# Holding splits back behind evictions in an expert layer, with down weights loaded as row pairs

## The chip, the cores and the metric

The kernel runs on one core of a Trainium2 chip. A core has five engines with queues of their own, which meet through semaphores: TensorE (PE, matrix products and transposes into PSUM), VectorE (DVE), ScalarE (ACT), GpSimd (POOL) and SyncE (SP, which here issues loads). Sixteen DMA engines move data between HBM and SBUF. The metric is the device time of one execution in microseconds, lower is better.

## What is computed

A trunk of two layers over 256 tokens of width 1024, all in float32. Each layer has a mixer (three attention-like branches); layer 0 then has a dense feed-forward block and layer 1 a mixture of 8 experts. The change touches the experts alone:

```python
def swiglu(h, w_gate_up, w_down):
    gt, up = jnp.split(h @ w_gate_up, 2, axis=-1)
    return (jax.nn.silu(gt) * up) @ w_down

def moe_swiglu(h, w_router, w_gate_up, w_down):   # D_FF_EXPERT = 3584, N_EXPERTS = 8, TOP_K = 2
    ...
    for e in range(N_EXPERTS):
        y = y + combine[:, e:e + 1] * swiglu(t, w_gate_up[e], w_down[e])
```

## The kernel before

**Two parts for each weight.** To keep float32 precision a weight slab is split: ACT copies it to a rounded high part (`exp_hi`, L1104), DVE subtracts that from the raw slab to get the low part (`exp_lo`, L1618), and PE multiplies with both.

**Slots.** The experts run in slots, one expert each. A slot gathers the tokens of its expert, multiplies, and scatters the result. Slots 0, 1, 3, 5, 7 are big (up to 128 tokens; three products per weight tile: hi x hi, hi x lo, lo x hi, `passes`, L1895 to L1897). Slots 2, 4, 6 are small (`few`, up to 64 tokens): there the tokens' high and low parts lie side by side in one operand, so PE needs two products per tile (L2231, L2232), and the half that holds the low part is folded in by `low` on ACT and `fold_low` on PE. In this data there are 8 slots; the last one is a turn of a loop that is written for up to 11.

**Slabs.** The weights of an expert come as 42 slabs of 128 x 2048 float32, 1 MiB each. An expert's hidden width is cut in four steps, three of 1024 columns and one (step 3) of 512. The order of the slabs, from 0, is: step 0 gate (0 to 3) and up (4 to 7); step 1 gate (8 to 11) and up (12 to 15), down of step 0 (16 to 19); step 2 gate and up (20 to 27), down of step 1 (28 to 31); step 3 gate (32, 33) and up (34, 35), down of step 2 (36 to 39), down of step 3 (40, 41). SP loads them into 14 raw places in turn (L555); a load waits until PE has used the slab 14 before. The high parts have a ring of 6 places (`EXP_RING`): ACT may split slab j once PE has used slab j - 6, its "holder". The numbering runs on over slots: slab 0 of a slot follows slab 41 of the one before.

**Evictions.** Beside splits, ACT and DVE carry the results on: `silu` (ACT, L1147) and the product with the up half, `hidden` (DVE, `hs`, L1744); `hidden_hi` and `hidden_lo` (`hts`, L1154 and L1753), which take the transposed hidden values out of PSUM, and `hts_end` for step 3; `y_hi` (L1165) and `output_lo` (L1711) for the result of the slot before; `add_slot` (`xs`, L1719) after the scatter; `tokens_hi` and `tokens_lo` (`xg`, L1116 and L1640) for the tokens of the next slot. PE transposes `hs` in `turn_hidden` (L2260) once DVE has made it (`e_h`), and in a small slot `block(1, 1, ...)`, the up product of step 1, waits for the `hs` of step 0 too, because it writes where DVE reads.

**What sets the order.** ACT and DVE run the same hand-written program: `uses(n)` counts slabs that PE will have used (`used`), and at each count `expert_split` puts in all splits that are allowed by then: those whose holder is below `used - LATE`. An eviction stands where the count reaches the slabs it needs, and waits for PE there. With `LATE` = 1 the splits up to slab `used` + 4 stand ahead of it in the queue. An instruction that waits holds up all that is queued behind it on its engine.

**Loads of the down weights.** Slab q of the down matrix takes 256 rows of 1024 columns. Partition p gets the rows p and 128 + p of them, each 4 KB, as two k-tiles. PE transposes `hs[:, a*P:(a+1)*P]` to make the matching hidden columns a k-tile.

Of the kernel before, what the change touches and what calls it, by code (L numbers as in the profile page):

```python
# [30 lines left out]
P = 128  # L31
# [25 lines left out]
EXP_SLAB = 2048  # L57
EXP_RAW, EXP_RING, LATE = 14, 6, 1

# [39 lines left out]
def is_first(i):  # L99
    return type(i) is int and i == 0  # L100


# [93 lines left out]
def trunk(nc, x_in, mem_in, mix_norm_g, w_in, sb_q_g, sb_k_g, gla_a_up, gla_a_b, gla_o_g, ca_q_g,  # L196
# [10 lines left out]
    with ExitStack() as ctx:  # L207
# [315 lines left out]
        def _(sp):  # L523
# [12 lines left out]
            def expert_slabs(e, i):  # L536
                gate_up = moe_gate_up[0].rearrange("e (k p) n -> e p k n", p=P)
                down = moe_down[0].rearrange("e (k p) n -> e p k n", p=P)
                j = 0

                def load(src, n):
                    nonlocal j
                    if not is_first(i) or j >= EXP_RAW:
                        sp.wait_ge(slab_used, i * EXP_SLABS + (PRE + j - EXP_RAW + 1))
                    if j == W_RAW_SLOT:
                        sp.wait_ge(lo_ready, PRE)
                    if j == GATES_SLOT:
                        sp.wait_ge(norm_done, NT * (3 * LAYERS))
                    if j == XT_SLOT:
                        sp.wait_ge(slab_used, PRE)  # L550
                    if j == HN_SLOT:
                        sp.wait_ge(gathered, 1)
                        sp.wait_ge(h_stored, 16)
                    dst = exp_slots[j % EXP_RAW].rearrange("p (k n) -> p k n", k=n)
                    sp.dma_start(dst, src).then_inc(more_ready[j % EXP_RAW], 16)  # L555
                    j += 1

                def cols(c, w):
                    n = EXP_SLAB // w
                    for k in range(0, KT, n):  # L560
                        load(gate_up[bass.ds(e, 1), :, k:k + n, c:c + w]
                             .rearrange("e p k n -> p (e k) n"), n)

                def rows(s):
                    c, w = STEP[s]
                    n = EXP_SLAB // DM
                    for k in range(c // P, (c + w) // P, n):
                        load(down[bass.ds(e, 1), :, k:k + n, :].rearrange("e p k n -> p (e k) n"),
                             n)

                for s, (c, w) in enumerate(STEP):
                    cols(c, w)
                    cols(D_EXP + c, w)
                    if s > 0:
                        rows(s - 1)
                rows(STEPS - 1)
# [239 lines left out]
        def _(act):  # L816
# [275 lines left out]

            def expert_split(i, few, used):

                nonlocal j
                while j < EXP_SLABS:
                    if RINGS[few][j] is not None:
                        place, holder = RINGS[few][j]
                        if holder >= used - LATE:
                            return  # L1100
# [20 lines left out]

            def expert(i, few, next_few, folds=0):
                nonlocal j
# [3 lines left out]
                def uses(n):  # L1127
                    nonlocal used
                    for _ in range(n):
                        used += 1  # L1130
                        expert_split(i, few, used)

# [29 lines left out]
                if not is_first(i):  # L1162
                    expert_split(i, few, 0)
                    act.wait_ge(slab_used, at + PRE)
# [40 lines left out]
            for i in range(1, 7, 2):  # L1205
                expert(i, False, True)
                expert(i + 1, True, False, i * STEPS)
            with act.Fori(7, slots) as i:
                expert(i, False, False)
            act.wait_ge(slab_used, slots * EXP_SLABS + PRE)  # L1210
# [5 lines left out]
        def _(dve):  # L1216
# [392 lines left out]

            def expert_split(i, few, used, at_most=EXP_SLABS):  # L1610
                nonlocal j
                while j < at_most:
                    if RINGS[few][j] is not None:
                        place, holder = RINGS[few][j]
                        if holder >= used - LATE:
                            return
# [5 lines left out]

            expert_split(0, False, 0, 1)
            link(dve.memset(slot_pos, 0.0))
# [98 lines left out]

            def expert(i, few, next_few, folds=0):
                nonlocal j
# [3 lines left out]
                def uses(n):  # L1729
                    nonlocal used  # L1730
                    for _ in range(n):
                        used += 1
                        expert_split(i, few, used)
                        if is_first(i):
# [33 lines left out]
                if not is_first(i):  # L1768
                    expert_split(i, few, 0)
                    output_lo(i)  # L1770
# [51 lines left out]
            for i in range(1, 7, 2):  # L1822
                expert(i, False, True)
                expert(i + 1, True, False, i * STEPS)
            with dve.Fori(7, slots) as i:
                expert(i, False, False)
            for c in range(2):
# [8 lines left out]
        def _(pe):  # L1836
# [385 lines left out]
            def expert(i, few, folds=0):  # L2222
# [25 lines left out]
                def fold_low(s, up):  # L2248
# [5 lines left out]
                    ins.then_inc(low_folded, 1)  # L2254

                def turn_hidden(s):
                    pe.wait_ge(e_h, i * STEPS + (s + 1))
                    dst = ps[:, DM:2 * DM] if s < STEPS - 1 else pa[:, BW:2 * BW]
                    for a in range(STEP[s][1] // P):
                        ins = pe.transpose(dst[:, a * P:(a + 1) * P], hs[:, a * P:(a + 1) * P],  # L2260
                                           ident[:, :])
# [117 lines left out]
```

## Time and profile before

| | us |
|---|---|
| median of 3 runs | 1708.3 (1707.7 to 1708.5) |
| profiled execution | 1706.9 |
| its span | 1705.0 |
| experts (from the first `exp_hi` to the end) | about 766 to 1705 |
| slot 4, small | about 1248 to 1351 |
| slot 5, big | about 1351 to 1473 |

The span is what the trace covers, from its first instruction to its last; a few microseconds lie around it. In the rows further down, a timeline row has its start, its duration, the engine, the line and what it writes and reads, and in brackets how long the engine had been idle before and who released it. Instructions overlap a little in an engine: the next one starts about 0.1 us before the last one's end, so work is counted from start to start.

### The profile page before, as it was taken

The page shows a single profiled execution, that of the slowest core. Times are in us where ns is not written, and L with a number is a line of the kernel's source. Part 1 is how long each engine was busy: PE and PEld are TensorE (multiplying, and loading weights), DVE is VectorE, ACT ScalarE, POOL GpSimd, SP SyncE. Part 2 cuts the span into 40 slices and gives each one's busy share as a digit, 9 for nine tenths or more (in the row PEclk, how much of TensorE's full clock was granted, in tenths as well). Part 3 has the DMA queues.
Part 4 walks back from the last instruction along what each step waited for, and adds up shares of the span by engine and source line. Part 5 has one row for each costly group of instructions (what it writes and reads, how often), then busy time and mean ns, then how long its engine had stood idle before and what let it go on. Part 6 is the DMA issues. An engine that isn't in the chain of part 4 may idle for free.

```text
span 1705.0 us, 20144 instructions
## 1 busy us (share of the span) xinstructions
PE 1627.2 (95%) x7594; PEld 1332.1 (78%) x7594; DVE 1305.4 (77%) x965; ACT 1108.9 (65%) x950; POOL 104.5 (6%) x123
## 2 busy tenths in 40 slices
PE   7999998999999999978999998899989899988998
PEld 5777886888887778867888887688877788876886
DVE  6654666555666546658989889999899998999985
ACT  5547554444555565536777778887698877887773
POOL 4111000000012110000200000000000000000000
PEclk9999999999999999998999999999999999999999
DMA  8544444656565544487999999999999999999990
GB/s 275 179 142 147 149 148 154 216 184 187 175 209 162 148 149 148 148 322 265 370 384 354 377 367 401 400 409 405 386 381 396 409 409 403 384 403 409 409 385 26
DMA packets 161335, 484.84 MB, mean 284 GB/s; under 512 B 12992, under 2 KB 15072, under 8 KB 161248
## 3 DMA queue, kind: packets, MB, share of 16 engines
q1 hardware_dynamic: 158112, 474.16, 76.2%
q0 software_dynamic: 3136, 9.48, 1.6%
q8 instruction: 60, 0.98, 0.2%
q14 instruction: 27, 0.22, 0.0%
HBM read 481.50 MB, written 2.10 MB: 284 GB/s over the span
## 4 chain that ended last, share of the span: by engine, by line
PE 83%; DVE 11%; issue 2%; ACT 2%; POOL 1%; DMA 0%; DVEq 0%; POOLq 0%; ACTq 0%
PE pa L1895 18%; PE pa L1897 18%; PE pa L1896 18%; PE ps L1997 5%; DVE exp_lo_a L1618 5%; PE ps L1895 4%; PE ps L1897 4%; PE ps L1896 4%; PE pa L2231 3%; PE pa L2232 3%; DVE exp_lo_b L1618 2%; PE ps L2260 1%; PE ps L2231 1%; PE ps L2232 1%; POOL hrs L697 1%
## 5 line engine op out<-in xcount | busy, mean ns | idle before, releaser
L1618 DVE TENSOR_TENSOR exp_lo_a<-exp_raw_a,exp_hi 128x2048 fp32r<-128x2048 f32 x240 | 538.3, 2287 | 35.2 <-ACT exp_hi L1104 34.9
L1104 ACT ACTIVATE exp_hi<-exp_raw_a 128x2048 fp32r<-128x2048 f32 x240 | 451.4, 1918 | 90.9 <-PE pa L1897 50.0
L1232 DVE TENSOR_TENSOR w_lo<-w_raw,w_hi 128x1024 fp32r<-128x1024 f32 (+2 forms) x229 | 277.4, 1226 | 135.8 <-ACT w_hi L830 126.9
L830 ACT ACTIVATE w_hi<-w_raw 128x1024 fp32r<-128x1024 f32 (+2 forms) x229 | 237.3, 1050 | 171.7 <-PE pa L1897 147.6
L1895 PE MATMUL pa<-w_hi,r 128*128 128x512 f32 x600 | 240.0, 400 | 0.0
L1897 PE MATMUL pa<-w_hi,r 128*128 128x512 f32 x600 | 234.0, 390 | 0.0
L1896 PE MATMUL pa<-w_lo,r 128*128 128x512 f32 x600 | 233.8, 390 | 0.0
L1618 DVE TENSOR_TENSOR exp_lo_b<-exp_raw_b,exp_hi 128x2048 fp32r<-128x2048 f32 x96 | 217.9, 2288 | 15.4 <-ACT exp_hi L1104 14.5
L1895 PE MATMUL pa<-exp_hi,xg 128*128 128x512 f32 x560 | 220.4, 394 | 3.4 <-issue 3.4
L1897 PE MATMUL pa<-exp_hi,xg 128*128 128x512 f32 x560 | 218.7, 391 | 0.0
L1104 ACT ACTIVATE exp_hi<-exp_raw_b 128x2048 fp32r<-128x2048 f32 x96 | 182.6, 1918 | 31.6 <-PE pa L1897 23.6
L2231 PE MATMUL pa<-exp_hi,xg 128*128 128x512 f32 x336 | 139.6, 415 | 14.2 <-issue 14.2
L1896 PE MATMUL pa<-exp_lo_a,xg 128*128 128x512 f32 x380 | 148.4, 390 | 0.0
L1895 PE MATMUL pa<-w_hi,xt 128*128 128x512 f32 (+1 forms) x320 | 124.2, 388 | 9.5 <-DVE xt L1268 9.5
L1895 PEld LDWEIGHTS pa<-w_hi,r 128*128 128x128 f32 x600 | 112.7, 188 | 25.6 <-issue 2.0
L1897 PEld LDWEIGHTS pa<-w_hi,r 128*128 128x128 f32 x600 | 112.6, 188 | 24.3
L1896 PEld LDWEIGHTS pa<-w_lo,r 128*128 128x128 f32 x600 | 112.8, 188 | 21.9
L1895 PEld LDWEIGHTS pa<-exp_hi,xg 128*128 128x128 f32 x560 | 105.5, 188 | 24.8 <-issue 3.6
L1897 PE MATMUL pa<-w_hi,xt 128*128 128x512 f32 (+1 forms) x320 | 122.8, 384 | 0.0
L1897 PEld LDWEIGHTS pa<-exp_hi,xg 128*128 128x128 f32 x560 | 105.4, 188 | 22.1
L1896 PE MATMUL pa<-w_lo,xt 128*128 128x512 f32 (+1 forms) x320 | 122.6, 383 | 0.0
L1895 PE MATMUL ps<-exp_hi,hts 128*128 128x512 f32 x240 | 94.5, 394 | 0.0
(299 smaller groups left out, 2269.4 us busy)
## 6 DMA issues: line engine op xcount, KB each, us to landing
exp_raw_a<-in_moe_w_gate_up SPq DMA_DIRECT2D x152, 1024.0 KB, 9.6
exp_raw_a<-in_moe_w_down SPq DMA_DIRECT2D x88, 1024.0 KB, 8.9
exp_raw_b<-in_moe_w_gate_up SPq DMA_DIRECT2D x72, 1024.0 KB, 8.4
w_raw<-in_w_in SPq DMA_DIRECT2D x104, 512.0 KB, 4.3
exp_raw_b<-in_moe_w_down SPq DMA_DIRECT2D x24, 1024.0 KB, 8.7
w_raw<-in_ff_w_gate_up SPq DMA_DIRECT2D x44, 512.0 KB, 4.5
w_raw<-in_ff_w_down SPq DMA_DIRECT2D x22, 512.0 KB, 3.5
w_raw<-in_w_mem_kv SPq DMA_DIRECT2D x16, 512.0 KB, 5.8
```

What stands on the lines that cost most here:

```text
L697: pool.tensor_tensor(dst[:, 0:n], src[:, 0:n], half[:, 0:n], ALU.pow)\
L830: act.activation(w_hi[:, s % SPLIT, 0:n], raw_slot(s)[:, 0:n], ACT.Copy)\
L1104: act.activation(exp_hi[:, place, :], exp_slots[j % EXP_RAW], ACT.Copy)\
L1232: dve.tensor_tensor(w_lo[:, s % SPLIT, 0:w], raw_slot(s)[:, 0:w], w_hi[:, s % SPLIT, 0:w].bitcast(F32), ALU.subtract)\
L1618: dve.tensor_tensor(exp_lo[j % EXP_RAW], exp_slots[j % EXP_RAW], exp_hi[:, place, :].bitcast(F32), ALU.subtract)\
L1895: pe.matmul(dst, hi, m_hi, start=first, stop=False)
L1896: pe.matmul(dst, hi, m_lo, start=False, stop=False)
L1897: return pe.matmul(dst, lo, m_hi, start=False, stop=last)
L1997: return pe.matmul(dst, a, b, start=start, stop=stop, skip_group_check=True)
L2231: pe.matmul(dst, src[:, 0, k, :], m_hi, start=first, stop=False)
L2232: return pe.matmul(dst, src[:, 0, k, :], m_lo, start=False, stop=last)
L2260: ins = pe.transpose(dst[:, a * P:(a + 1) * P], hs[:, a * P:(a + 1) * P], ident[:, :])
```

## The change

Three edits, all in the experts.

1. `LATE` is replaced by a number that depends on the slot and on `used`. A split is put in while its holder is below `used - late`, so with `late` = L the splits up to slab `used` + 5 - L are ahead of an eviction. In a small slot L is 1 up to `used` = 9, 2 to 19, 3 to 29, 4 to 39 and 5 at the end. In a big slot behind a small one it is 5 up to `used` = 7, 4 to 15, 3 to 23, 2 to 31 and then 1. Slots 0 and 1 keep 1.
2. A down slab gives partition p the neighbouring rows 2p and 2p + 1 of its 256, one run of 8 KB.
3. To match, `turn_hidden` transposes columns with a step of two: for an even a the even columns of a block of 256, for an odd a the odd ones.

```diff
+def holds_back(few, after_few, used):
+
+    if few:
+        return 1 + used // 10
+    return max(1, 5 - used // 8) if after_few else 1
...
-                down = moe_down[0].rearrange("e (k p) n -> e p k n", p=P)
+                down = moe_down[0].rearrange("e (q p k) n -> e p q (k n)", p=P, k=EXP_SLAB // DM)
...
-                    n = EXP_SLAB // DM
-                    for k in range(c // P, (c + w) // P, n):
-                        load(down[bass.ds(e, 1), :, k:k + n, :].rearrange("e p k n -> p (e k) n"),
-                             n)
+                    n = EXP_SLAB // DM * P
+                    for q in range(c // n, (c + w) // n):
+                        load(down[bass.ds(e, 1), :, q:q + 1, :].rearrange("e p q n -> p (e q) n"),
+                             1)
...
-            def expert_split(i, few, used):
+            def expert_split(i, few, used, late=1):
...
-                        if holder >= used - LATE:
+                        if holder >= used - late:
...
-                        expert_split(i, few, used)
+                        expert_split(i, few, used, holds_back(few, after_few, used))
...
-                    expert_split(i, few, 0)
+                    expert_split(i, few, 0, holds_back(few, after_few, 0))
...
-                expert(i, False, True)
+                expert(i, False, True, after_few=i > 1)
...
-                expert(i, False, False)
+                expert(i, False, False, after_few=True)
...
+                row_pairs = hs[:, :].rearrange("p (q c k) -> p q k c", c=P, k=EXP_SLAB // DM)
...
-                        ins = pe.transpose(dst[:, a * P:(a + 1) * P], hs[:, a * P:(a + 1) * P],
+                        ins = pe.transpose(dst[:, a * P:(a + 1) * P], row_pairs[:, a // 2, a % 2, :],
```

The edits of `expert_split` and of `uses` are made alike in ACT's and in DVE's program. Instructions are neither added nor taken away.

DVE, the end of small slot 4 and the start of big slot 5. `exp_lo` rows are splits, L1744 is `hs` (1024 wide for step 2, 512 for step 3), L1711 is `output_lo`, L1719 is `add_slot`. Before:

```order
L1618 TENSOR_TENSOR exp_lo_a<-exp_raw_a,exp_hi 128x2048 x6
L1618 TENSOR_TENSOR exp_lo_b<-exp_raw_b,exp_hi 128x2048
L1618 TENSOR_TENSOR exp_lo_a<-exp_raw_a,exp_hi 128x2048
L1744 TENSOR_TENSOR hs<-pa,hs 128x1024
L1618 TENSOR_TENSOR exp_lo_a<-exp_raw_a,exp_hi 128x2048 x2
L1753 TENSOR_TENSOR hts<-ps,hts 128x8x64
L1618 TENSOR_TENSOR exp_lo_b<-exp_raw_b,exp_hi 128x2048 x2
L1744 TENSOR_TENSOR hs<-pa,hs 128x512
L1618 TENSOR_TENSOR exp_lo_b<-exp_raw_b,exp_hi 128x2048
L1753 TENSOR_TENSOR hts_end<-pa,hts_end 128x4x64
L1640 TENSOR_TENSOR xg<-ps,xg 128x1024
L1618 TENSOR_TENSOR exp_lo_a<-exp_raw_a,exp_hi 128x2048 x5
```

And now (the lines of the file are 7 further down):

```order
L1625 TENSOR_TENSOR exp_lo_a<-exp_raw_a,exp_hi 128x2048 x6
L1751 TENSOR_TENSOR hs<-pa,hs 128x1024
L1625 TENSOR_TENSOR exp_lo_a<-exp_raw_a,exp_hi 128x2048
L1625 TENSOR_TENSOR exp_lo_b<-exp_raw_b,exp_hi 128x2048
L1760 TENSOR_TENSOR hts<-ps,hts 128x8x64
L1625 TENSOR_TENSOR exp_lo_a<-exp_raw_a,exp_hi 128x2048 x2
L1751 TENSOR_TENSOR hs<-pa,hs 128x512
L1625 TENSOR_TENSOR exp_lo_a<-exp_raw_a,exp_hi 128x2048
L1760 TENSOR_TENSOR hts_end<-pa,hts_end 128x4x64
L1647 TENSOR_TENSOR xg<-ps,xg 128x1024
L1625 TENSOR_TENSOR exp_lo_b<-exp_raw_b,exp_hi 128x2048 x3
```

Ahead of the `hs` of step 2 stood splits up to slab 36, now up to 33; ahead of `hts_end` up to 41, now up to 38.

ACT at the same seam: `exp_hi` rows are splits, L1165 is `y_hi`, which waits for slab 41 of the small slot, and the L1147 behind it is `silu` of step 0 of the big slot, which waits for slab 3. Before:

```order
L1154 ACTIVATE hts_end<-pa 128x4x64
L1104 ACTIVATE exp_hi<-exp_raw_a 128x2048 x5
L1165 ACTIVATE hts<-ps 128x1024
L1104 ACTIVATE exp_hi<-exp_raw_a 128x2048 x2
L1104 ACTIVATE exp_hi<-exp_raw_b 128x2048
L1104 ACTIVATE exp_hi<-exp_raw_a 128x2048
L1147 ACTIVATE hs<-pa 128x1024
```

And now:

```order
L1161 ACTIVATE hts_end<-pa 128x4x64
L1111 ACTIVATE exp_hi<-exp_raw_b 128x2048 x3
L1111 ACTIVATE exp_hi<-exp_raw_a 128x2048
L1172 ACTIVATE hts<-ps 128x1024
L1111 ACTIVATE exp_hi<-exp_raw_a 128x2048 x4
L1154 ACTIVATE hs<-pa 128x1024
```

Ahead of `y_hi` stood the splits of slabs 0 to 4 of the big slot, now that of slab 0 alone (the three ahead of it are 39 to 41 of the small slot); ahead of `silu` slabs up to 8, now up to 4.

## Rows read from the trace of the kernel before

**Rows 1.** The page, section 1: busy us, share of the span, instructions.
```profile
PE 1627.2 (95%) x7594; PEld 1332.1 (78%) x7594; DVE 1305.4 (77%) x965; ACT 1108.9 (65%) x950; POOL 104.5 (6%) x123
```

**Rows 2.** PE's waits, 780 to 1705 us: total us, times, longest us.
```profile
PE ps L2260 <- DVE hs L1744: 16.9, 3, 5.6
PE pa L2231 <- issue: 14.2, 3, 4.8
PE pa L1895 <- issue: 3.4, 1, 3.4
```

**Rows 3.** DVE's timeline, slot 4: start, us, instruction, [idle before].
```profile
1240.14 11.10 DVE L1618 TENSOR_TENSOR exp_lo_a<-exp_raw_a,exp_hi 128x2048 fp32r<-128x2048 f32 x5 [1.00 <-ACT exp_hi L1104]
...
1276.69 1.22 DVE L1744 TENSOR_TENSOR hs<-pa,hs 128x1024 f32<-128x1024 f32 x1
...
1289.37 4.49 DVE L1618 TENSOR_TENSOR exp_lo_a<-exp_raw_a,exp_hi 128x2048 fp32r<-128x2048 f32 x2 [1.66 <-ACT exp_hi L1104]
...
1313.30 13.29 DVE L1618 TENSOR_TENSOR exp_lo_a<-exp_raw_a,exp_hi 128x2048 fp32r<-128x2048 f32 x6
...
1342.40 2.29 DVE L1618 TENSOR_TENSOR exp_lo_b<-exp_raw_b,exp_hi 128x2048 fp32r<-128x2048 f32 x1 [0.18 <-ACT exp_hi L1104]
1344.61 0.42 DVE L1753 TENSOR_TENSOR hts_end<-pa,hts_end 128x256 fp32r<-128x256 f32 x1
...
1346.07 11.09 DVE L1618 TENSOR_TENSOR exp_lo_a<-exp_raw_a,exp_hi 128x2048 fp32r<-128x2048 f32 x5
```

**Rows 4.** PE's timeline, slots 4 and 5.
```profile
1278.01 0.76 PE L2231 MATMUL pa<-exp_hi,xg 128*128 128x512 f32 x1 [4.74 <-issue]
...
1304.93 1.04 PE L2260 MATMUL ps<-ident,hs 128*128 128x128 f32 x8
1305.73 0.48 PE L2231 MATMUL pa<-exp_hi,xg 128*128 128x512 f32 x1
...
1309.90 0.39 PE L2231 MATMUL pa<-exp_hi,xg 128*128 128x512 f32 x1
...
1313.30 0.39 PE L2232 MATMUL pa<-exp_lo_b,xg 128*128 128x512 f32 x1
...
1361.77 1.98 PE L1997 MATMUL ps<-hts,selT 128*128 128x512 f32 x8
1363.58 0.39 PE L1895 MATMUL pa<-exp_hi,xg 128*128 128x512 f32 x1
```

**Rows 5.** ACT's waits, 800 to 1700 us, the longest of eleven.
```profile
ACT exp_hi L1104 <- PE pa L1897: 62.2, 76, 1.8
```

**Rows 6.** Line 1711, `output_lo`, once a slot: ns min/median/max, first and last start.
```profile
L1711 DVE TENSOR_TENSOR hts<-ps,hts x7: 1216/1219/1220, 906.4 to 1581.0; 128x1024 fp32r<-128x1024 f32 x7
```

**Rows 7.** ACT's timeline, slot 4 and the start of slot 5.
```profile
1281.86 1.91 ACT L1104 ACTIVATE exp_hi<-exp_raw_a 128x2048 fp32r<-128x2048 f32 x1 [4.39 <-PE pa L2232]
...
1344.07 9.12 ACT L1104 ACTIVATE exp_hi<-exp_raw_a 128x2048 fp32r<-128x2048 f32 x5
1353.08 1.02 ACT L1165 ACTIVATE hts<-ps 128x1024 fp32r<-128x1024 f32 x1
1353.98 3.72 ACT L1104 ACTIVATE exp_hi<-exp_raw_a 128x2048 fp32r<-128x2048 f32 x2
...
1361.97 1.03 ACT L1147 ACTIVATE hs<-pa 128x1024 f32<-128x1024 f32 x1 [0.66 <-PE pa L1897]
```

**Rows 8.** By stretch: us, PE, PEld, DVE, ACT, POOL busy, PEclk, DMA share, GB/s.
```profile
782.70:786.00 3.30, 3.29 (x9) 2.64 (x10) 2.56 (x5) 0.00 (x0) 0.00 (x0) 0.57 0.28 113
1278.00:1285.00 7.00, 6.99 (x19) 5.48 (x20) 7.00 (x6) 1.91 (x1) 0.00 (x0) 0.58 1.03 410
1300.00:1308.00 8.00, 8.00 (x41) 6.72 (x40) 8.00 (x6) 8.00 (x7) 0.99 (x1) 1.00 1.05 393
1316.00:1340.00 24.00, 18.18 (x79) 14.05 (x78) 24.00 (x13) 17.83 (x14) 0.00 (x0) 0.93 1.03 410
```

**Rows 9.** Line 555, the loads issued from 1325 to 1330 us.
```profile
L555 SPq DMA_DIRECT2D exp_raw_a<-in_moe_w_gate_up x2: 2154/2154/2154, 1325.2 to 1327.6; - x2
...
DMA to landing us min/median/max: 18.5/18.5/18.6
```

More of the change, by code:

```diff
@@ L57 @@
 EXP_SLAB = 2048
-EXP_RAW, EXP_RING, LATE = 14, 6, 1
+EXP_RAW, EXP_RING = 14, 6
 FF_BLOCKS = [(c, min(BW, D_FF - c)) for c in range(0, D_FF, BW)]
@@ L1120, in _, with expert @@
             tokens_hi(1, False)
-            def expert(i, few, next_few, folds=0):
+            def expert(i, few, next_few, folds=0, after_few=False):
                 nonlocal j
@@ L1608, in _, with expert_split @@
             j = 0
-            def expert_split(i, few, used, at_most=EXP_SLABS):
+            def expert_split(i, few, used, late=1, at_most=EXP_SLABS):
                 nonlocal j
@@ L1614, in expert_split @@
                         place, holder = RINGS[few][j]
-                        if holder >= used - LATE:
+                        if holder >= used - late:
                             return
@@ L1621, in expert_split @@
                     j += 1
-            expert_split(0, False, 0, 1)
+            expert_split(0, False, 0, at_most=1)
             link(dve.memset(slot_pos, 0.0))
@@ L1722, in add_slot, with expert @@
                         .then_inc(added, 1)
-            def expert(i, few, next_few, folds=0):
+            def expert(i, few, next_few, folds=0, after_few=False):
                 nonlocal j
@@ L1732, in uses @@
                         used += 1
-                        expert_split(i, few, used)
+                        expert_split(i, few, used, holds_back(few, after_few, used))
                         if is_first(i):
@@ L1768, in expert @@
                 if not is_first(i):
-                    expert_split(i, few, 0)
+                    expert_split(i, few, 0, holds_back(few, after_few, 0))
                     output_lo(i)
@@ L1822, in _ @@
             for i in range(1, 7, 2):
-                expert(i, False, True)
+                expert(i, False, True, after_few=i > 1)
                 expert(i + 1, True, False, i * STEPS)
             with dve.Fori(7, slots) as i:
-                expert(i, False, False)
+                expert(i, False, False, after_few=True)
             for c in range(2):
```

## The prediction

> **What bounds the kernel now.** The profiled execution took 1706.9 us for a span of 1705.0, beside a median of 1708.3 in the runs, so I work out a difference in the span and put it on 1708.3. The page's first section [rows 1] shows a busy TensorE (PE) for the whole span; a busy PE is not yet a bound, so the waits come next. In the experts PE waits in few places [rows 2]: once for 3.4 us at their start, and in each of the three small slots twice: 4.7 us (14.2 in all) at `block(1, 1, ...)` and 5.6 us (16.9) at `turn_hidden(2)`. The first is called "issue", but PE stands there before `e_h`, and it resumes at 1278.01 [rows 4], 0.1 us after DVE's `hidden(0)` ends (1276.69, 1.22 us) [rows 3]. So both stalls have one form: DVE's product `hs` stands in its queue behind splits of slabs that PE does not need yet. No wait of ACT in the experts names a DMA [rows 5]: no weight load is late.
>
> The second thing to read is DVE in the same slot [rows 3]. From 1240.14 (slab 0) to 1346.07 it is idle for 1.66 and 0.18 us alone. Six splits take 13.29 us, 2.20 apart. PE needs 0.227 us a matmul (1309.90 to 1313.30 for 15 steps) [rows 4], so 8 of them, 1.81 us, for a slab in a small slot, and 12, 2.72 us, in a big one. **A small slot is DVE's, a big one is PE's.** A stall of PE in a small slot is therefore mostly slack which it would have to spend elsewhere waiting for splits, and its length is not what removing it is worth. A pair of slots lasts (1581.0 - 906.4) / 3 = 224.9 us [rows 6].
>
> **The small slot after the change.** I follow slot 4; all three small slots show the same two stalls. With `late` = 1, DVE has split up to slab used + 4 when it comes to an eviction; with `late` = L up to used + 5 - L. That moves one split (2.2 us) behind `hidden(0)` and three (6.6 us) behind `hidden(2)`. No split is added or taken away.
> - Stall 1: `hs` starts at 1276.69 - 2.20 = 1274.5, PE resumes at 1275.8 and not at 1278.0. At full clock it does 2 slabs, one fold (0.45) and 8 transposes (0.9) by 1280.9, where it was 1286.0 before. ACT's wait of 4.39 us for PE ahead of slab 18 [rows 7] shrinks, and DVE's 1.66 us before slab 18 is gone: gain 1.7 us on DVE.
> - Stall 2: the six splits from 1313.30 are slabs 29 to 34, so slab 33 was split at 1324.3; now at 1324.3 - 1.7 = 1322.6, `hs` follows at once, PE ends slab 33 at 1324.6 and turns with no stall. What is late next is each split: 34 at 1325.9, 35 at 1328.1, after `hts` (half a `xg`, 0.6) 36 and 37 at 1330.9 and 1333.1. PE, which took 34 to 36 from stock before, now follows DVE at 2.2 us a slab.
> - End: `hs` of step 3 (0.6), 38, then `hts_end` and `xg`, 39, 40, 41. In the trace split 41 ends at 1344.6 [rows 3]. To this add those two evictions, which are now ahead of it (1346.07 - 1344.61 = 1.46), subtract the two idle times (1.84): 1344.2, and with 0.1 us of hand-over PE ends slab 41 at 1346.2.
> - Before: `hs` at 1361.97 waited for slab 3 of the next slot [rows 7], so PE ended it at 1361.8, and slab 41 four slabs earlier, at 1350.9. **Lead at the seam: 4.7 us.** It can't be the 10.4 us of both stalls, since DVE's sum ends there.
>
> **The big slot after it.** `late` starts at 5 here, and each eviction that must wait for PE now has little behind it in stock. The trace of before has no such wait, so I price it by the durations of its steps.
> - used = 0: only slab 0 is split (1346.5; PE starts it 0.3 late). ACT's `y_hi` (0.92 to its next instruction [rows 7]) waits for slab 41 and slab 1's high part stands behind it: 1346.2 + 0.1 + 0.9 + 1.9 + 0.1 = 1349.2, low part 2.2: 1351.4. PE has been done with slab 0 since 1349.3: **a new stall of 2.1 us**. Before, five slabs lay ready ahead of `y_hi` (1346.07, x5).
> - used = 4: ACT's `silu(0)` waits for slab 3, DVE's `add_slot` for the scatter (8 matmuls, 1.81 us [rows 4]) with only slab 4 split. Behind the second half's scatter come 0.1 + 1.25 + 2.2 = 3.6 us, PE has slab 4 for 2.7: stall 0.9, with the start of DVE's first addition counted 1.2.
> - used = 12: slabs 12 and 13 are ready, `hts` hi, `silu`, hi 14 and lo 14 follow the transposes by 1.0 + 0.9 + 1.9 + 2.3 + 0.1 = 6.2 us against 5.4 of PE: stall 0.7.
> - used = 16 on: at least 2 slabs ahead and cheaper waits, DVE gains 0.5 us a slab: nothing.
>
> Of 4.7 us, 0.3 + 2.1 + 1.2 + 0.7 = 4.3 are given back: **0.4 us a pair, 1.3 us in all.** The big slot is PE's, so what is left of the lead goes through to the end.
>
> **Clock.** Behind the 3.4 us stall PE was granted 0.57 of its clock (near 1.2 GHz) for some 3 us, behind stall 1 0.58 [rows 8]; seven matmuls at 0.43 and not 0.227 cost 1.4 us. Stall 1 is now 2.5 us, the new one 2.1. For these I take nothing as the centre and 1.4 us each as the end of the range; in the small slot such a dip also restores up to 1.7 us of DVE's idle time.
>
> **Loads.** 14 of 42 loads of a slot read 8 KB rows in place of two 4 KB rows; their number, order and semaphores stay. Streaming 4 KB rows the engines moved 410 GB/s at share 1.03; where 2 KB rows (step 3) were among them 393 at 1.05 [rows 8]. If doubling once more gave as much again, a load of 2.56 us would fall by 0.11, 112 loads by 12 us of DMA time. None of it is on the path: the loads issued from 1325.2 to 1327.6 landed 18.6 us later at the latest [rows 9], by 1346.2, and are slabs 4 and 5 of the next slot, which ACT reached at 1351.3 and 1354.0 [rows 7]. The change reaches slab 4 near 1352.7. A pair moves 84 slabs of 1 MiB (128 x 2048 fp32), 215 us at 410 GB/s, under 224.9. So 0. What the trace can't exclude is that the row pairs are slower; they may be so by some 7 us of lag before ACT sees it. The Trainium skill (Perfetto Trace Analysis, DMA Optimizations) says that batching from 2 to 4 or 8 KB can dramatically improve throughput, when DMA-bound. By that rule up to the 12 us above would be gained; ACT's waits say that its condition isn't met, and it is a rival below.
>
> **Transposes.** 28 a slot read every second column of `hs`. Eight contiguous ones take 0.80 us to the next matmul (1304.93 to 1305.73) [rows 4]. No row of the kernel has a strided operand on PE. Ends: 0, and double, 0.1 us each, 28 x 5 big slots = 14 us (in small ones DVE hides it). I take 0, as only the weight load's read changes, and it overlaps matmuls. The Trainium skill (SBUF — State Buffer, Door 1: The DMA port swizzle) states 16-byte lines with at least two hits each for full rate: a step of two fp32 has exactly two, so by the page it costs nothing; no run here shows it yet.
>
> **Rivals.**
> - *Lead kept.* If the hold-back in big slots hardly bites (ACT or DVE further ahead than my walk has them, other hand-overs), 4.4 us a pair stay: -13 us, 1695. Half of it: 1702. For: before, not one stall of PE in a big slot after the first. Against: the order puts `y_hi` behind one split. Chance 0.25.
> - *Loads bind* in a way that no row names: all 12 us of DMA time come off, 1696. For: the engines are at share 1.03 for most of a small slot. Against: the releasers. Chance 0.02.
> - *Slower: stalls at the seam.* The stalls of 2.1 and 1.2 us cut PE's clock in the PE-bound slot, and the dip at stall 1 gives DVE its 1.7 us of idle back: 0.4 - 1.4 - 0.5 - 1.7 = -3.2 a pair, +10 us: 1718; with one of these, 1712. It decides once the dips cost over 0.4 us a pair. For: rows 8 after 3.4 us. Against: nothing shows a dip after 2 us. Chance 0.20.
> - *Strided transposes at half rate:* +14: 1721. Chance 0.06.
> - *The change doesn't do what it says* (the splits are held back, but some other wait is behind the stalls): 1708.3, inside the forecast's own range and chance.
>
> **How the numbers follow.** Forecast 0.47: 1708.3 - 1.3 = 1707. Its own range is 1702 to 1711 (0.5 us either way on each of three stalls a pair). 0.2%, 3.4 us, is about what a measurement can tell. Faster: lead kept 0.25, loads 0.02, plus 0.07 of the forecast: 0.34. Slower: 0.20 + 0.06 less 0.02: 0.24. Within: 0.42. For 8 in 10 the range goes from 1697 (most of the kept lead) to 1715 (most of the seam's price).
>
> **What would show it.** PE's waits for `hs`: 5.6 us x3 gone, the unnamed one 4.7 to 2.5. Small slots with PE at 2.2 us a slab to the end. Slab 41 of slot 4 ended 4.7 us earlier relative to its start. Then new PE waits in slots 3, 5 and 7: about 2 us before the second slab and 1 us at the sixth. A pair of 224.5 us. ACT's waits with no DMA, down loads landing no later. `hs` transposes at 0.8 us for eight. I am wrong if big slots show no new wait (then near 1695), if PE's clock falls at the seams, or if a DMA is named as releaser.

## The result

The changed kernel takes 1717.2 us (median of 5 runs, 1716.19 to 1717.58); the kernel before took 1708.27 beside it (1707.38 to 1708.51). The ratio is 1.0054, interval 1.0042 to 1.0066: slower by 9 us, where I had forecast 1 us faster and a range up to 1715. The profiled execution has a span of 1715.4 us against 1705.0. What stands ahead of the first transposes of `hs` in slot 0 varies by up to 4.5 us from one traced execution to another, whatever the kernel (they start between 816.5 and 821.0 us); so where I compare traces below, a "lag" is a start time less that in the kernel before, both counted from those transposes.

In the new file all names of the text keep their names, and their lines move by 7 or 9: splits L1104 and L1618 are L1111 and L1625, `y_hi` L1165 is L1172, `output_lo` L1711 is L1718, `hidden` L1744 is L1751, transposes L2260 are L2269.

The page of the changed kernel, section 1, answers to [rows 1]: the same instructions, and PE busy for 7 us more with no matmul added.
```profile
PE 1634.5 (95%) x7594; PEld 1328.8 (77%) x7594; DVE 1303.7 (76%) x965; ACT 1105.3 (64%) x950; POOL 104.4 (6%) x123
```
PE's waits in the experts, which answer to [rows 2] (us in total, times, longest):
```profile
PE pa L1902 <- DVE exp_lo_a L1625: 12.5, 10, 2.5
PE pa L2238 <- issue: 7.5, 3, 2.5
PE ps L2238 <- DVE exp_lo_b L1625: 5.9, 5, 1.9
PE pa L1902 <- issue: 4.9, 1, 4.9
```
The waits for `hs` (16.9 us) are gone and the unnamed ones fell from 4.7 to 2.5, both as forecast. In their place stands PE's wait for low parts in the big slots (12.5), and a second kind (5.9) that I had not priced, at the last slabs of the small slots. PE's timeline at the seam from slot 4 to slot 5 has all of them:
```profile
1345.28 0.50 PE L2238 MATMUL ps<-exp_hi,hts 128*128 128x512 f32 x1 [1.83 <-DVE exp_lo_b L1625]
1345.61 0.40 PE L2239 MATMUL ps<-exp_lo_b,hts 128*128 128x512 f32 x1
...
1346.48 0.63 PE L2238 MATMUL ps<-exp_hi,hts 128*128 128x512 f32 x1
1346.91 0.63 PE L2239 MATMUL ps<-exp_lo_b,hts 128*128 128x512 f32 x1
1347.34 0.63 PE L2238 MATMUL ps<-exp_hi,hts 128*128 128x512 f32 x1
...
1357.88 0.50 PE L1902 MATMUL pa<-exp_hi,xg 128*128 128x512 f32 x1 [2.53 <-DVE exp_lo_a L1625]
...
1366.17 1.98 PE L2004 MATMUL ps<-hts,selT 128*128 128x512 f32 x8
...
1372.01 0.50 PE L1902 MATMUL pa<-exp_hi,xg 128*128 128x512 f32 x1 [1.14 <-DVE exp_lo_a L1625]
```
The reader is to see three things: slab 39 waits 1.83 us; from 1346.48 the matmuls start 0.43 us apart and not 0.23; then slab 1 of the big slot waits 2.53 us and slab 5 waits 1.14. Slab 14 waits 0.67 (not shown). The other two seams have 2.10 and 2.14, 1.14 and 1.27, 0.67 and 0.67.

ACT's timeline at the same seam, answering to [rows 7]:
```profile
1346.40 1.89 ACT L1111 ACTIVATE exp_hi<-exp_raw_a 128x2048 fp32r<-128x2048 f32 x1
1352.67 1.03 ACT L1172 ACTIVATE hts<-ps 128x1024 fp32r<-128x1024 f32 x1 [4.38 <-PE ps L2239]
1353.60 7.31 ACT L1111 ACTIVATE exp_hi<-exp_raw_a 128x2048 fp32r<-128x2048 f32 x4
1366.37 1.03 ACT L1154 ACTIVATE hs<-pa 128x1024 f32<-128x1024 f32 x1 [5.47 <-PE pa L1904]
```
and DVE's, answering to [rows 3]:
```profile
1349.55 2.28 DVE L1625 TENSOR_TENSOR exp_lo_a<-exp_raw_a,exp_hi 128x2048 fp32r<-128x2048 f32 x1
1353.73 1.23 DVE L1718 TENSOR_TENSOR hts<-ps,hts 128x1024 fp32r<-128x1024 f32 x1 [1.90 <-ACT hts L1172]
1355.53 8.90 DVE L1625 TENSOR_TENSOR exp_lo_a<-exp_raw_a,exp_hi 128x2048 fp32r<-128x2048 f32 x4 [0.57 <-ACT exp_hi L1111]
1367.28 2.48 DVE L1726 SCALAR_TENSOR_TENSOR xs<-ps,small,xs 128x1024 f32<-128x1024 f32 x2 [2.85 <-PE ps L2004]
```
Before, five slabs were split ahead of `y_hi`, and ACT came to it with PE done. Now ACT stands 4.38 us before it with one slab behind it in stock, DVE stands 1.90 us, and both then split slab 1 while PE waits: the walk of the prediction for `used` = 0, step by step. DVE stands idle for 5.3 us at this seam in all (1.90, 0.57 and 2.85).

By stretch, answering to [rows 8] (us, busy times, PEclk, DMA share, GB/s):
```profile
1346.00:1350.00 4.00, 4.00 (x13) 3.10 (x12) 4.00 (x3) 2.30 (x2) 0.00 (x0) 0.57 1.02 409
1130.00:1134.00 4.00, 4.00 (x12) 3.14 (x13) 4.00 (x2) 2.89 (x2) 0.00 (x0) 0.63 1.02 409
1585.00:1588.00 3.00, 3.00 (x9) 2.33 (x8) 3.00 (x3) 1.51 (x1) 0.00 (x0) 0.51 1.03 410
1372.00:1376.00 4.00, 3.99 (x17) 3.30 (x18) 4.00 (x2) 4.00 (x3) 0.00 (x0) 1.00 1.02 423
```
The first three are one stretch from each seam: PE was granted 0.51 to 0.63 of its full clock there, so for most of each stretch it was at the lower of its two levels, 1.2 and not 2.4 GHz. I counted the 512-column matmuls that start about 0.43 us apart, from slot 2 on, and what they take over 0.227 us. **Before there were five such dips, 9.0 us in sum, every one inside a small slot, where PE has slack. In the changed kernel there are six, 8.7 us, but three of them, 4.5 us, lie at the seams** (1131 to 1134: 1.40; 1346 to 1349: 1.57; 1585 to 1588: 1.55). Two of these stand in the PE-bound big slot, behind the wait for slab 1. The one at 1346 stands in the last slabs of the small slot, behind the wait for slab 39, and is hidden in part: it cost about 0.9 us (see the lead at slab 41 below). The time at the low clock did not grow; it moved to where it is paid for.

### The profile page after: what moved, and what is told of

Read it like the earlier page. It is cut to its first block, busy times and chain, and to the rows that moved or that the text cites. A ratio compares the mean times of both kernels' runs of the same rounds, so it can differ in the third digit from the quotient of the medians.

```text
span 1715.4 us, 20144 instructions
## 1 busy us (share of the span) xinstructions
PE 1634.5 (95%) x7594; PEld 1328.8 (77%) x7594; DVE 1303.7 (76%) x965; ACT 1105.3 (64%) x950; POOL 104.4 (6%) x123
## 4 chain that ended last, share of the span: by engine, by line
PE 80%; DVE 12%; ACT 3%; issue 3%; POOL 1%; DMA 0%; DVEq 0%; ACTq 0%; POOLq 0%
PE pa L1902 18%; PE pa L1904 17%; PE pa L1903 17%; DVE exp_lo_a L1625 6%; PE ps L2004 5%; PE ps L1902 4%; PE ps L1904 4%; PE ps L1903 4%; PE pa L2238 3%; PE pa L2239 3%; DVE exp_lo_b L1625 2%; ACT exp_hi L1111 1%; PE ps L2269 1%; POOL hrs L704 1%; PE ps L2238 1%
## 5 line engine op out<-in xcount | busy, mean ns | idle before, releaser
L1625 DVE TENSOR_TENSOR exp_lo_a<-exp_raw_a,exp_hi 128x2048 fp32r<-128x2048 f32 x240 | 537.4, 2285 | 31.5 <-ACT exp_hi L1111 31.3
L1111 ACT ACTIVATE exp_hi<-exp_raw_a 128x2048 fp32r<-128x2048 f32 x240 | 448.4, 1913 | 51.2 <-PE pa L1904 30.1
L1902 PE MATMUL pa<-exp_hi,xg 128*128 128x512 f32 x560 | 223.2, 399 | 17.5 <-DVE exp_lo_a L1625 12.5
L1625 DVE TENSOR_TENSOR exp_lo_b<-exp_raw_b,exp_hi 128x2048 fp32r<-128x2048 f32 x96 | 216.8, 2286 | 9.5 <-ACT exp_hi L1111 9.2
L1111 ACT ACTIVATE exp_hi<-exp_raw_b 128x2048 fp32r<-128x2048 f32 x96 | 181.3, 1914 | 24.5 <-PE pa L1904 16.5
```

What stands on the lines that cost most here:

```text
L1111: act.activation(exp_hi[:, place, :], exp_slots[j % EXP_RAW], ACT.Copy)\
L1625: dve.tensor_tensor(exp_lo[j % EXP_RAW], exp_slots[j % EXP_RAW], exp_hi[:, place, :].bitcast(F32), ALU.subtract)\
L1902: pe.matmul(dst, hi, m_hi, start=first, stop=False)
```

## The experiments

**Which part does it.** Four kernels from the changed one: the row pairs alone (no hold-back), the hold-back alone, and the hold-back in one kind of slot alone. The runs below were timed in three sets, each beside the kernel before, which took 1707.57, 1707.58 and 1708.17 us in them; so medians of different sets compare to about 0.6 us.

*Row pairs and strided transposes alone (rows_only).* Edit, against the changed kernel:
```
-    if few:
-        return 1 + used // 10
-    return max(1, 5 - used // 8) if after_few else 1
+    return 1
```


> Edits 2 and 3 alone (8 KB row pairs and transposes with a step of two; every eviction has the splits of before ahead of it). Theory: the rise to 1717.2 is the hold-back's; the strided transposes cost 0.08 us for eight, as the changed kernel's slots 0 and 1 show (a lag of 1.33 us at the end of two slots, 0.66 of it at the start), so 8 slots give about +2 us over before: 1710 to 1711. Rival A (the row pairs speed up the loads, and loads matter): below 1708. Rival B (the row pairs or the stride carry most of the rise): 1714 or more.

Measured: 1711.06 (1709.53 to 1712.02; before 1707.57), ratio 1.0017 (1.0009 to 1.0026). Lag at the last scatter 3.0 us. They cost something.

*Hold-back alone (hold_only).* Edit, with the load's lines of the kernel before likewise:
```
-    ins = pe.transpose(dst[:, a * P:(a + 1) * P], row_pairs[:, a // 2, a % 2, :],
+    ins = pe.transpose(dst[:, a * P:(a + 1) * P], hs[:, a * P:(a + 1) * P],
```


> Edit 1 alone, with the 4 KB rows and contiguous transposes of before. Theory (edits add): 1717.2 less the 2 us of edits 2 and 3: about 1715. Rival A (8 KB rows help where the engines are saturated): 1717 or more. Rival B (the stride hurts in the PE-bound seams): 1710.

Measured: 1716.0 (1710.24 to 1716.94), ratio 1.0037 (1.0024 to 1.0051), final lag 5.9. Most of the loss is the hold-back's. The two edits do not simply add: alone they cost 8.4 and 3.5 us, together 8.9. The six runs also lie apart: two took 1710.2 and 1711.5 us at a mean granted clock of 0.989 and 0.990, four took 1715.8 to 1716.9 at 0.986 to 0.988. This fits dips at the seams that come in some executions and not in others, but only one of the six has a trace (1716.2; dips at 1132 and 1347, none at the third seam), so it is not shown.

*Small slots alone (small_only).* Edit:
```
-    return max(1, 5 - used // 8) if after_few else 1
+    return 1
```


> The changed kernel with the hold-back in small slots alone; big slots have the splits of before. Theory (the stalls at slab 1, 5 and 14 of the big slots come from holding back there): PE's lead of 2.4 us at slab 41 is kept in each of three pairs, less 0.3 for transposes, and the 1.3 us of slots 0 and 1 stay: about 1703, no new wait of PE in slots 3, 5, 7. Rival (DVE has no stock at the end of a small slot, and the stalls come from that whatever the big slot does): 1708 to 1714 with waits at slab 1 still there.

Measured: 1698.21 (1697.98 to 1699.35), ratio 0.9945 (0.9932 to 0.9958). Against rows_only this is 12.9 us less, 4.3 a pair, close to the forecast's lead of 4.7 and more than I expected here. PE's waits have the small slots' two kinds, and of the big slots' only one of 0.2 us:
```profile
PE pa L2238 <- issue: 7.5, 3, 2.5
PE ps L2238 <- DVE exp_lo_b L1625: 6.0, 5, 1.9
PE pa L1902 <- issue: 4.2, 1, 4.2
```
The lead does go through to the end when nothing takes it. This is what the rival "lead kept" said, with the hold-back in big slots removed rather than harmless.

*Big slots alone (big_only).* Edit:
```
     if few:
-        return 1 + used // 10
+        return 1
```


> The changed kernel with the hold-back in big slots alone. Theory: each of three seams costs a stall of about 2.5 us at slab 1, 1.3 at slab 5 and 1.0 at slab 14 with the restart, nothing is gained in small slots, 1.5 to 2 us for the transposes: 1708.3 + 14.4 + 2 = about 1725. Rival (the seams stall only because small slots end without stock): about 1710.

Measured: 1731.05 (1730.17 to 1731.3), ratio 1.0136 (1.0121 to 1.015): 20.0 us over rows_only, 6.7 a seam, as the changed kernel is 19.0 over small_only, 6.3 a seam. The three parts nearly add up: +3.5 for the rows, -12.9 small, +20.0 big make +10.6; measured 9. Its trace has the low clock at 1366 and 1598, in slots 5 and 7, behind waits of 2.53 us for slab 1, beside that of its small slots; behind the same wait of 2.53 us in slot 3 it has none.

**Which part of the big slots' schedule.** The prediction priced 2.1 + 0.3 at slab 1 and 1.2 + 0.7 later. Two kernels add one or the other to small_only:
```
-    return 1
+    return 5 if after_few and used == 0 else 1                     # seam_first
+    return max(1, 5 - used // 8) if after_few and used > 0 else 1  # seam_rest
```
*Only at used = 0 (seam_first).* 

> small_only, and in the big slots behind small ones a hold-back at their very start alone (late = 5 at used = 0, then 1). Theory: the wait of PE ahead of slab 1 (2.1 us), its restart and the clock dip behind it in the PE-bound slot cost 3.5 us a seam where the lead was kept: 1698.2 + 3 x 3.5 = 1708.7, and PE has no wait at slabs 5 and 14. Rival: only the named wait is lost, without the clock: 1698.2 + 3 x 2.1 = 1704.5. Other rival: what is not split ahead of slab 1 is missing later as well, and slab 5 stalls even at late = 1: up to 1712.

Measured: 1708.62 (1707.48 to 1710.46), 10.4 over small_only, 3.5 a seam. PE's timeline has the wait ahead of slab 1 at each seam (2.06, 2.09, 2.11) and none at slabs 5 and 14. The first two:
```profile
1130.13 0.50 PE L1902 MATMUL pa<-exp_hi,xg 128*128 128x512 f32 x1 [2.06 <-DVE exp_lo_a L1625]
...
1352.47 0.50 PE L1902 MATMUL pa<-exp_hi,xg 128*128 128x512 f32 x1 [2.09 <-DVE exp_lo_a L1625]
```
Behind the second the clock fell, behind the first it didn't, as the stretches show (PEclk is the third number from the end):
```profile
1130.00:1134.00 4.00, 3.87 (x17) 3.23 (x18) 4.00 (x3) 4.00 (x3) 0.00 (x0) 1.00 1.03 410
1354.00:1358.00 4.00, 4.00 (x12) 3.18 (x11) 4.00 (x3) 4.00 (x3) 0.00 (x0) 0.58 1.03 410
```
In this one execution the seams cost 2.0, 3.9 and 2.3 us of lag (small_only's subtracted), 8.3 in all: where the clock stayed up the price is the wait itself or little more, where it fell some 1.6 more. (The 2.0 of the first seam is a little low, since small_only has a dip of 1.4 us of its own just ahead of it.) So about 2.1 us is the floor of a seam and 3.5 what the timed runs give, where the prediction had 2.4.

*The rest of the schedule (seam_rest).* 

> small_only, and in the big slots behind small ones the changed kernel's hold-back from used = 1 on (5 - used // 8), with late = 1 at used = 0. Theory: seam_first took 3.47 us a seam of small_only's gain; the rest of the schedule costs the waits at slabs 5 and 14 with their restart, 1.45 + 1.0 = 2.5 us a seam: 1698.2 + 3 x 2.5 = 1705.7. PE's waits in slots 3, 5 and 7: none at slab 1, about 1.1 at slab 5, 0.7 at slab 14. Rival: the stall at slab 5 grows, because at used = 1 to 4 nothing is split and the stock of five slabs is eaten by then as before: same 1705.7 but all of it at slab 5; or without the stall at slab 1 PE reaches slab 5 earlier and waits 2 us more there: up to 1710.

Measured: 1705.61 (1705.02 to 1708.77), 7.4 over small_only, 2.5 a seam. PE's waits at the first seam:
```profile
1145.42 0.50 PE L1902 MATMUL pa<-exp_hi,xg 128*128 128x512 f32 x1 [1.14 <-DVE exp_lo_a L1625]
...
1172.12 0.50 PE L1902 MATMUL pa<-exp_hi,xg 128*128 128x512 f32 x1 [0.67 <-DVE exp_lo_a L1625]
```
The waits named sum to 1.8 and the lag rises by 2.4 to 2.5 across them: each such wait costs some 0.3 us beyond its own length. I read no cause for this in the trace. The prediction had 1.9 for both.

The lags of after against small_only give the same split in one pair of traces: 3.5, 4.0 and 4.1 us up to the scatter behind slab 1 at the three seams, then 2.4, 2.4 and 2.5 across slabs 5 and 14.

**Which half of the row pairs.** The loads alone and the transposes alone, both with `late` = 1.

*Loads (pairs_load_alone).* 

> late = 1 everywhere. The down weights are loaded as row pairs of 8 KB, but PE still transposes contiguous columns of hidden, so each column meets the weight rows of another one: the experts' second product is of permuted rows, its amount of work unchanged. Theory: no load is waited for, so the loads give nothing: 1707 to 1708.5, the time before. Rival 1: the 8 KB rows carry the 3 us that rows_only lost, then 1711. Rival 2: loads bind unseen, then under 1705. Weight loads of the transposes 141 ns and eight transposes in 0.80 us as before; fewer packets (147 thousand in place of 161).

Measured: 1708.32 (1707.25 to 1710.66; before 1707.58), ratio 1.0003 (0.9994 to 1.0012); lag in the PE-bound slots 0 and 1 is 0.00. From 1140 to 1150 us, with 8 KB rows among them, the loads move 419 GB/s in this run and 409 in the kernel before (423 in the last stretch shown above, against 410 [rows 8]), and it is worth nothing, for no one waits for a load. The Trainium skill (Perfetto Trace Analysis, DMA Optimizations) ties its advice to being DMA-bound; this run shows the other side of that condition.

*Transposes (stride_alone).* 

> late = 1 everywhere. The transposes of hidden read every second column, the down weights come in 4 KB rows as before, so each column meets the weight rows of another one: the experts' second product is of permuted rows, its amount of work unchanged. Theory: the strided weight load (207 ns in place of 141) makes eight transposes 0.08 us longer and four 0.04; 28 of them in each of five big slots give 1.4 us, and the rest of rows_only's 3 us (ACT and DVE, too, wait for the end of the transposes in every slot) makes it 1709.5 to 1711. Rival: the transposes cost nothing outside their own rows, then 1708.3. Eight transposes in 0.87 us, packets 161 thousand.

Measured: 1711.77 (1710.25 to 1712.16), ratio 1.0019 (1.001 to 1.0029). The lag grows by 0.34 us in every one of slots 0 and 1 and by 0.26 to 0.34 in slots 3, 5 and 7: 1.6 us in all, the price of the transposes themselves. The rest of its 3.3 us of final lag came in the small slots; there this execution lost 11.1 us at the low clock where the one of before lost 9.0. That the strided reads caused these I can't show, though rows_only has 10.6 and the loads alone 8.8. PE's weight loads for the transposes in the changed kernel (ns min/median/max, first and last start in us):
```profile
L2269 PEld LDWEIGHTS ps<-ident,hs x192: 195/209/209, 817.5 to 1682.8; 128*128 128x128 f32 x192
```
and in the kernel before:
```profile
L2260 PEld LDWEIGHTS ps<-ident,hs x192: 138/141/231, 816.8 to 1672.4; 128*128 128x128 f32 x192
```
In the changed kernel's PE timeline eight transposes take 0.86 us to the next matmul, in place of 0.80 [rows 4]; in slot 0 the lag rises by 0.10 across each eight. The rows that follow are from slot 4:
```profile
1306.83 1.11 PE L2269 MATMUL ps<-ident,hs 128*128 128x128 f32 x8
1307.69 0.47 PE L2238 MATMUL pa<-exp_hi,xg 128*128 128x512 f32 x1
```
The Trainium skill (SBUF — State Buffer, Door 1: The DMA port swizzle) gives full rate for two hits in a 16-byte line, as a step of two fp32 has. For PE's weight load of this kernel the measurement says otherwise: 209 ns, not 141.

**Can it be had without the loss?** The rest keep small_only's hold-back, with loads and transposes as in the kernel before.

*The base (small_only_4k).* 

> The splits are held back in the small slots alone (1 + used // 10), loads and transposes of hidden stay as in the kernel before. With small_only at 1698.2 and the two row edits costing about 3 us where they were changed alone (1711.1 against 1707.6, and 17 to 14 in the pair of changed kernel and hold_only), this gives 1695.5 if the costs add. Rival: in the small slots DVE hides PE's transposes and the part that is PE-bound gives less than 3 us, then 1697 to 1698. PE's waits as in small_only: 2.5 us x3 ahead of block(1, 1), none for hs, 0.7 and 1.8 us at the last slabs of the small slots, none in slots 3, 5 and 7.

Measured: 1696.33 (1695.27 to 1698.76), ratio 0.9933 (0.992 to 0.9947): 1.9 under small_only, between theory and rival; in the two traces the final lags differ by 1.95.

```
     if few:
-        return 1 + used // 10
+        return 3 if 8 <= used < 12 else 1 + used // 10   # early_hs0_4k
+        return 3 if used >= 36 else 1 + used // 10       # even_end_4k; both_4k has both
```
*Stall 1 taken away too (early_hs0_4k).* 

> small_only_4k, with late = 3 in the small slots for used 8 to 11, which takes one more split (2.2 us) out from ahead of the first hs. Theory: PE's wait at block(1, 1) goes from 2.5 to about 0.3, and DVE's idle 0.6 us ahead of slab 18 goes; PE is not the bound there, so the gain is that idle time alone, 0.6 us a pair, at most 1 us with the clock no longer falling: 1696.3 - 1.8 = 1694.5 (1693.3 to 1695). Rival: as with both stalls in the kernel before, the wait is slack: 1696.3.

Measured: 1696.17 (1695.38 to 1697.66): nothing by the medians, as the rival had it. PE's waits, the first and the third largest:
```profile
PE ps L2238 <- DVE hts L1760: 7.0, 3, 2.3
...
PE pa L1902 <- issue: 5.0, 1, 5.0
```
and in its timeline the one in slot 4:
```profile
1281.59 0.50 PE L2238 MATMUL ps<-exp_hi,hts 128*128 128x512 f32 x1 [2.32 <-DVE hts L1760]
```
The wait at `block(1, 1)` fell from 2.5 to 0.3 and came back as 2.3 us a step later, for `hts`, which now has five splits between the first `hs` and itself, and not four. DVE's order of work changed, its sum didn't. In the traces the final lag is 1.0 us less all the same, as much as the idle time of DVE ahead of slab 18 that small_only_4k has in two of its small slots (0.49 and 0.53) and this kernel in none; the timed runs spread over more than that.

*A flat end (even_end_4k).* 

> small_only_4k, with late = 3 in place of 4 and 5 from used = 36 on in the small slots. It takes the waits of PE for a split at the last slabs of a small slot (0.7 and 1.8 us, behind which the clock fell) apart: one or two splits stand ahead of the last hs, hts and xg again. Theory: DVE's sum to slab 41 is the same, and what falls away is the clock dip behind the 1.8 us wait (8 to 10 matmuls at 0.43 us in place of 0.227, 1.2 us a pair, part of which DVE hides): 1696.3 - 3 x 0.7 = 1694. Rival: a wait for hs or for hts at the end takes its place (late = 1 had 5.6 us at step 2): 1696 to 1700.

Measured: 1694.46 (1692.11 to 1696.79). The median is 1.9 lower, near the theory's 2.3, but the runs of the two overlap, and the profiled execution is the fastest of the five. The 0.7 us wait is gone and the last one is 1.6; its trace has one stretch at the low clock from slot 2 on, 1.57 us, where small_only_4k has three, 4.6 us. The theory's reason holds in part at most: only one of those three stands at the end of a small slot. In the first two pairs neither trace has one there, and the lag still falls by 0.7 and 0.8 us; what is gone is DVE's idle time at the end of the slot, 0.27 to 0.29 us ahead of the last `hs` and 0.23 ahead of slab 39. In the third pair, where small_only_4k has two dips and this kernel none, it falls by 1.9.

*Both (both_4k).* 

> early_hs0_4k and even_end_4k together. If the two gains are of different waits they add: 1696.3 - 1.8 - 2.1 = 1692.4. Rival: the DVE's time saved at the first hs is given back at the end of the slot as a longer wait for PE: then the better of the two, 1694.

Measured: **1693.39 (1692.47 to 1694.16), ratio 0.9914 (0.9901 to 0.9928)**, the fastest of all: 15 us under the kernel before, 24 under the changed one. Its PE has no matmul at the low clock from slot 2 on. Its largest wait is again the 2.3 us for `hts`, three times, and no cost of it shows in the lags.

## Why the prediction was wrong

By its own sum: a lead of 4.7 us a pair from the small slots, 4.3 given back in the big one, nothing for clock and transposes: -0.4 a pair. From the runs: **-4.3 a pair in the small slots (rows_only to small_only), +6.3 in the big ones (small_only to after), and +3.5 in all for the rows and transposes**: 3 x 2.0 + 3.5 = 9.5. (These three steps lead from the kernel before to the changed one, so their sum is the measured difference by construction; beside each other the two kernels gave 8.9.) The mechanism and nearly every place of it were right. The step that failed is the price of a seam, 4.3 us in the sum and 6.3 measured, 6 us over the three seams; the largest part of that is the clock, which the sum put at nothing. The second is the term for the transposes, put at 0 and measured at 1.6 to 3.5 us. The lead, 4.7 in the sum and 4.3 measured, is the small rest.

- **Stall 1: right.** 4.74 to 2.50 us, and the clock dips behind it as before (1053, 1281, 1506), hidden but for this: DVE's idle ahead of slab 18 went from 1.66 to 0.60 and not to 0, because ACT was held by that same dip. small_only shows it: behind the same wait its slots 2 and 6 have the dip and 0.61 and 0.60 us of idle, its slot 4 has neither. DVE's row for slot 2, and the stretches behind the wait in slots 2 and 4 (PEclk 0.66 and 1.00):
```profile
1063.11 6.81 DVE L1625 TENSOR_TENSOR exp_lo_a<-exp_raw_a,exp_hi 128x2048 fp32r<-128x2048 f32 x3 [0.61 <-ACT exp_hi L1111]
...
1053.00:1058.00 5.00, 5.00 (x16) 3.92 (x16) 5.00 (x4) 1.96 (x2) 0.00 (x0) 0.66 1.03 410
1274.00:1281.00 7.00, 6.99 (x34) 5.93 (x35) 7.00 (x6) 3.80 (x5) 0.00 (x0) 1.00 1.03 411
```
- **Stall 2: right.** Gone; PE follows the splits. What I had not seen is the wait of 1.83 us for slab 39, with 0.69 before it. `late` is 4 and 5 there, so the last `hts`, `hts_end` and `xg` come with no stock behind them. I had the terms of DVE's sum right and did not ask what PE does between them.
- **Lead at slab 41: too large in the sum's terms.** In slot 4 of after `y_hi` starts 99.9 us after that of the slot's own start, where my walk gave 97.7: 1.1 us is DVE's idle time left (0.60, 0.27, 0.25), about 0.9 the clock dip at 1346; 0.2 stays unnamed. In the other two pairs it starts at 99.0 and 99.1, without a dip at the end; there the dip comes behind the slab 1 wait instead. Each pair paid for one.
- **Slab 1: right in size.** 2.1 forecast; 2.10, 2.53, 2.14 seen. The 0.3 for slab 0 was seen once in three seams, as 0.2.
- **Slabs 5 and 14: waits right, price short.** 1.2 and 0.7 forecast, 1.14 to 1.27 and 0.67 seen; the lag rose by 1.5 and 1.0 to 1.1.
- **Clock: the wrong step.** I wrote that nothing shows a dip after 2 us and took nothing as the centre, 1.4 as the end. All three seams had one, 1.4 to 1.57, 4.5 us in this trace, of which some 3.9 were paid (the one at 1346 cost 0.9). The timed runs price it a little lower: seam_first paid 3.5 us a seam where the waits alone were put at 2.4, so 1.1 a seam, 3.3 of the 10 us between forecast and result. It is not a fixed price: seam_first had the same wait three times and one dip. How often the clock falls behind such a wait is in the last section.
- **Loads: right.** Zero, for the reason given.
- **Transposes: wrong at the centre, inside the bounds.** Eight take 0.07 us longer to the next matmul and add 0.08 to 0.10 us of lag, where I took 0 and had 0.8 as the end; 1.6 us in all in the big slots, and up to 3.5 with what came in the small slots. The reason I gave for 0, that the longer weight load overlaps matmuls, did not hold.

The rival that came true is "slower: stalls at the seam" (1718 for all of it, chance 0.20). It named the cut clock in the PE-bound slot and its point of decision, 0.4 us a pair. That its figure lies within 1 us of the result is partly luck: it counted 1.7 us a pair of DVE's idle time given back, where 0.5 to 0.6 came, and it had nothing for the transposes, which cost 1.6 to 3.5 us in all. With stretches at half clock behind a 3.4 us and a 4.7 us wait in the very rows I quoted, and three forecast waits a seam, centre and end should have been nearer each other, and the range should have gone to 1718 at least.

One view that I had named in advance misled: the time between starts of `output_lo`. It is 224.0 us a pair in after against 224.9 in [rows 6], shorter in the slower kernel, because the change takes the splits out from ahead of `output_lo` in slot 7 but not in slot 1. The scatters of slots 1 and 7, which PE reaches in the same order in both, give 223.9 before and 226.1 after; and since the last of them stands ahead of the waits at slabs 5 and 14 of slot 7, even that is short: counted from behind slab 14 it is 223.9 and 226.9, the 3.0 us a pair that the medians show.

## What to carry to other kernels

Holding work back behind an eviction pays where the engine behind the eviction waits for it, and costs where it doesn't: here the same rule gave 4.3 us a pair in the slots that DVE bounds and took 6.3 in those that PE bounds, so set it by slot and test the halves apart. Price a new wait of TensorE in a stage that TensorE bounds with the time at half clock that may follow it (here 1.4 to 1.6 us, behind about half of the waits of 2.1 to 2.5 us), and a wait in a stage with slack at little: here the dips behind such waits cost 0.5 to 0.9 us. And follow the queue to the stage's end: the last evictions need stock as well.

## What the hardware showed

- TensorE's granted clock fell to its lower level behind waits as short as 1.8 to 2.1 us (1.83 with one of 0.69 shortly before it; 2.09 and 2.10 ahead of slab 1), for 6 to 8 matmuls of 512 columns, 0.43 us apart. The same wait of 2.06 us in the same kernel had no dip behind it. Counted over the traces: of the waits for slab 1 (2.06 to 2.53 us; after, hold_only, big_only, seam_first) 6 of 12 had a dip behind them, of those at `block(1, 1)` (2.49 to 2.54 us) 14 of 21, of those for slab 39 (1.78 to 1.88 us) 7 of 21, and of those of 1.6 us (6, in even_end_4k and both_4k) and of 1.1 to 1.3 us (12) none. What decides between one wait and another of the same length is open.
- A transpose whose columns lie two fp32 apart loads its weights in 209 ns in place of 141, and eight of them take 0.07 us longer to the next matmul and add about 0.1 us of lag where PE is the bound (0.34 us for 28).
- With 8 KB rows among them the loads moved 423 GB/s from 1372 to 1376 us and 419 from 1140 to 1150, where 4 KB rows alone moved 410 and 409.
